# First mixer of a two-block transformer kernel: l2 lengths as per-partition factors, denominators from a column of ones, turned outputs issued inside other work

## What is computed

```python
qkv = silu(causal_conv(pa[..., :1536], conv_w))
qa = l2norm(q of 4 heads of 128) * 128 ** -0.5      # x * rsqrt(sum(x * x) + eps)
ka = l2norm(k of 4 heads of 128)
oa = gated_delta_rule(qa, ka, va, g, beta)          # needs (I + L)^-1, L from ka, beta, decays
oa = rmsnorm(oa, norm_a) * silu(z)
# second half: mLSTM
num = pmat @ v ; den = sum(pmat, -1)
ob = rmsnorm(num / max(abs(den), exp(-m)), norm_b) * o_gate
out = concat(oa, ob) @ w_out
```

## Time and profile before

| | |
|---|---|
| profiled execution | 1546.2 us |
| its span | 1544.9 us |
| median of three runs | 1546.9 us |
| mean granted clock of PE | 0.967 |
| PE busy | 95% of the span |
| DVE, ACT, POOL busy | 65%, 50%, 7% |

### The profile page before, as it was taken

One profiled execution on the slowest core, in us unless ns is written; L12 is line 12 of the kernel. 1 busy time (PEld: TensorE's weight loads), 2 busy tenths in 40 slices (PEclk: granted clock), 3 DMA queues, 4 the chain that ended last, 5 costly groups with the idle time before them and its releaser, 6 DMA issues.

```text
span 1544.9 us, 26112 instructions
## 1 busy us (share of the span) xinstructions
PE 1466.5 (95%) x10914; PEld 1388.4 (90%) x10914; DVE 1007.5 (65%) x1517; ACT 766.4 (50%) x1192; POOL 113.6 (7%) x104
## 2 busy tenths in 40 slices
PE   5999998999999898999999998999999998999999
PEld 5988987999997687999998787899999787899999
DVE  4746558664478756764476775677756676577763
ACT  4433345444356344444456767544346666544343
POOL 0002311110001001110000000011100000011100
PEclk8989998999999998999999998999999997999999
DMA  8531234655544324655555321556565412255563
GB/s 267 145 101 55 77 115 129 199 181 181 185 163 164 109 83 140 192 188 174 186 170 171 120 103 34 161 164 190 172 207 194 151 67 83 82 164 175 183 196 103
DMA packets 186389, 228.91 MB, mean 148 GB/s; under 512 B 5920, under 2 KB 161056, under 8 KB 186144
## 3 DMA queue, kind: packets, MB, share of 16 engines
q1 hardware_dynamic: 185264, 222.47, 44.9%
q0 software_dynamic: 1008, 4.77, 0.9%
HBM read 226.18 MB, written 1.05 MB: 147 GB/s over the span
## 4 chain that ended last, share of the span: by engine, by line
PE 70%; DVE 17%; ACT 8%; issue 3%; DMA 0%; POOL 0%; ACTq 0%; SPq 0%; DVEq 0%; POOLq 0%
PE bank L494 20%; PE bank L495 19%; PE bank L496 19%; DVE weights_low L788 6%; ACT weights_high L682 3%; PE bank L997 2%; PE bank L502 2%; ACT S L2050 2%; PE bank L1995 1%; DVE cv L2853 1%; PE bank L1974 1%; DVE S L2125 1%; DVE cv L2850 1%; DVE cv L1398 1%; DVE pad L2840 1%
## 5 line engine op out<-in xcount | busy, mean ns | idle before, releaser
L788 DVE TENSOR_TENSOR weights_low<-weights_raw,weights_high 128x1024 fp32r<-128x1024 f32 (+3 forms) x421 | 505.4, 1222 | 307.5 <-ACT weights_high L682 307.2
L682 ACT CAST weights_high<-weights_raw 128x1024 fp32r<-128x1024 f32 (+3 forms) x421 | 424.0, 1030 | 268.1 <-PE bank L496 267.8
L494 PE MATMUL bank<-hT_high,weights_high 128*128 128x256 f32 (+1 forms) x1672 | 482.9, 289 | 24.8 <-DVE hT_low L867 8.9
L495 PE MATMUL bank<-hT_low,weights_high 128*128 128x256 f32 (+1 forms) x1672 | 478.5, 286 | 0.0
L496 PE MATMUL bank<-hT_high,weights_low 128*128 128x256 f32 (+1 forms) x1672 | 478.2, 286 | 0.0
L494 PEld LDWEIGHTS bank<-hT_high,weights_high 128*128 128x128 f32 (+1 forms) x1672 | 325.0, 194 | 31.7 <-issue 16.8
L495 PEld LDWEIGHTS bank<-hT_low,weights_high 128*128 128x128 f32 (+1 forms) x1672 | 325.3, 195 | 0.6
L496 PEld LDWEIGHTS bank<-hT_high,weights_low 128*128 128x128 f32 (+1 forms) x1672 | 324.9, 194 | 0.6
L494 PE MATMUL bank<-aT_high,weights_high 128*128 128x256 f32 x864 | 241.2, 279 | 0.2
L495 PE MATMUL bank<-aT_low,weights_high 128*128 128x256 f32 x864 | 240.6, 279 | 0.0
L496 PE MATMUL bank<-aT_high,weights_low 128*128 128x256 f32 x864 | 240.3, 278 | 0.0
(11 more groups left out here) (414 smaller groups left out, 1818.5 us busy)
## 6 DMA issues: line engine op xcount, KB each, us to landing
weights_raw<-in_w_up SPq DMA_DIRECT2D x32, 1024.0 KB, 5.4
weights_raw<-in_w_down SPq DMA_DIRECT2D x32, 1024.0 KB, 4.9
weights_raw<-in_ffn_w_gate SPq DMA_DIRECT2D x22, 1024.0 KB, 5.3
weights_raw<-in_ffn_w_up SPq DMA_DIRECT2D x22, 1024.0 KB, 5.3
...
```

Of the source, the lines that this page charges most:

```text
L494: k.E.matmul(out, xh, wh, start=first, stop=False)
L495: k.E.matmul(out, xh, wl, start=False, stop=False)
L682: k.A.copy(w.halves(n)[0], w.raw_part(n)).then_inc(*k.s.weight_high(n))
L788: k.V.tensor_tensor(low, w.raw_part(n), high.bitcast(F32), ALU.subtract).then_inc(*k.s.weight_low(n))
```

## The change

- The order of the ten feature panels is changed: keys first (512, 768), then queries, and values last. The kinds (convolution or not) stay in the same places. `CONV_AB` keeps the convolution buffers and POOL's squares in that order.
- The length sums come in two groups of eight, for the keys behind f3 and for the queries behind f6. Each has its own root on ACT and its own reciprocal on DVE. `l2T`, its transposes and the row products are gone, and so are the products that scaled queries and keys. In their place the length of the key in the row of `ab` is multiplied into beta, the products key x key and key x query are multiplied by the other key's length by partition (`over_lengths`), and the query's length goes into the outputs of a.
- `abT` moves from behind f4 to behind f5, the scan and the turned maxima from behind f6 to behind f7.
- The values of b get a column of ones, so that the weighted values have the denominator in column 128. L1145 and its step go. There are now four such products in four banks, two heads in each.
- The turned outputs of b are issued ahead of the first u product, into buffers of their own (`m.bT`). Those of a are issued in the 28th step of the output panels, that is four steps before the second ends.

```diff
@@ -45,11 +45,14 @@
-FEATURES_AB = [("qkv_a", 0), ("qkv_a", 256), ("qkv_a", 512), ("qk_b", COL_QB), ("qkv_a", 768), ("qk_b", COL_QB + 256),
+FEATURES_AB = [("qkv_a", 512), ("qkv_a", 768), ("qkv_a", 0), ("qk_b", COL_QB), ("qkv_a", 256), ("qk_b", COL_QB + 256),
...
+CONV_AB = [4, 6, 0, 2, 8, 10]
@@ -392,13 +395,13 @@
-    m.qkv, m.qkb, m.both_gates, m.vb = cut("qkv", 12, SEQ), cut("qkb", 8, SEQ), cut("both_gates", 2 * NT * 512), cut("vb", NT, 512)
+    m.qkv, m.qkb, m.both_gates, m.vb = cut("qkv", 12, SEQ), cut("qkb", 8, SEQ), cut("both_gates", 2 * NT * 512), cut("vb", NT, 4, P + 1)
...
-    m.l2, m.l2T, m.em = cut("l2", NT, 8), cut("l2T", SEQ), cut("em", NT, 4)
+    m.l2, m.em = [cut("l2", NT, 4) for _ in range(2)], cut("em", NT, 4)
@@ -407,6 +410,7 @@
+    m.bT = pair("bT", 4, SEQ)
@@ -1019,34 +1023,32 @@
     yield
+    tensor_square_lengths(k, 4)
+    yield
...
     yield
+    tensor_square_lengths(k, 0)
...
     E.transpose(bank[:, 8:16], m.mxT[0:8, P:SEQ], k.ident[0:8, 0:8]).then_inc(*s.products("ab mcol"))
-    bank = k.banks.fill("ab l2")
-    for c in range(8):
+    yield
+
+
+def tensor_square_lengths(k, c0):
+
+    E, s, m = k.E, k.s, k.ab
+    bank = k.banks.fill(("ab l2", c0))
+    for c in range(c0, c0 + 4):
...
             a = (c % 2) * SEQ + t * P
-            mm = E.matmul(bank[:, t * 8 + c:t * 8 + c + 1], m.sq[:, c // 2, a:a + P], k.ones[:, 0:1], start=True, stop=True)
-    mm.then_inc(*s.products("ab l2"))
-    yield
-    E.wait_ge(*s.inverse.at("ab l2"))
-    tensor_transposes(k, "ab l2T", [m.l2[:, t, :] for t in range(NT)])
-    yield
-    select = k.const("select").rearrange("p (h n) -> p h n", h=12)
-    E.wait_ge(*k.banks.was_read("ab l2T"))
-    for c in range(0, 8, 2):
-        bank = k.banks.fill(("ab l2 row", c))
-        E.matmul(bank[:, 0:SEQ], select[0:8, c, :], m.l2T[0:8, :], start=True, stop=True)
-        E.matmul(bank[:, SEQ:512], select[0:8, c + 1, :], m.l2T[0:8, :], start=True, stop=True).then_inc(*s.products(("ab l2 row", c)))
-    yield
+            mm = E.matmul(bank[:, t * 4 + c - c0:t * 4 + c - c0 + 1], m.sq[:, c // 2, a:a + P], k.ones[:, 0:1], start=True, stop=True)
+    mm.then_inc(*s.products(("ab l2", c0)))
@@ -1106,12 +1108,13 @@
             tensor_by_heads(k, ("ab Q", lv, j), lambda hd: m.C[j][:, hd, :], lambda hd: m.M[j][:, hd, :])
-        if lv == 1:
-            tensor_denominators(k)
         if lv == 2:
+            for hd in range(4):
+                E.wait_ge(*k.banks.was_read(("ab P", hd)))
...
                 E.wait_ge(*k.banks.was_read(("ab", COL_VB, t)))
-            tensor_weighted(k, ("ab h b", 0), m.PT, m.vb, 0)
+            E.wait_ge(*s.padding.at("ab ones"))
+            tensor_weighted_b(k, 0)
@@ -1122,11 +1125,13 @@
-            tensor_weighted(k, ("ab h b", 1), m.PT, m.vb, 1)
+            tensor_weighted_b(k, 1)
...
+    E.wait_ge(*s.mixed.at("b"))
+    tensor_feature_major(k, "ab b", m.mixed_b, 4)
@@ -1134,21 +1139,21 @@
-def tensor_denominators(k):
-    E, m = k.E, k.ab
-    for hd in range(4):
-        E.wait_ge(*k.banks.was_read(("ab P", hd)))
-    bank = k.banks.fill("ab den")
-    for t in range(NT):
-        for hd in range(4):
+def tensor_weighted_b(k, t):
...
+    m, n = k.ab, P + 1
+    for pair in range(2):
+        bank = k.banks.fill(("ab h b", t, pair))
+        for i in range(2):
+            hd = 2 * pair + i
...
-                mm = E.matmul(bank[:, t * 4 + hd:t * 4 + hd + 1], m.PT[:, hd, (t + u) * P:(t + u + 1) * P], k.ones[:, 0:1], start=(u == 0), stop=(u == t))
-    mm.then_inc(*k.s.products("ab den"))
+                mm = k.E.matmul(bank[:, i * n:(i + 1) * n], m.PT[:, hd, (t + u) * P:(t + u + 1) * P], m.vb[:, u, hd, :], start=(u == 0), stop=(u == t))
+        mm.then_inc(*k.s.products(("ab h b", t, pair)))
...
-    E, m = k.E, k.ab
+    E, s, m = k.E, k.s, k.ab
@@ -1159,6 +1164,11 @@
+    yield
+    for _ in range(19):
+        yield
+    E.wait_ge(*s.mixed.at("a"))
+    tensor_feature_major(k, "ab a", m.mixed_a, 4)
@@ -1189,15 +1199,10 @@
             next(side, None)
-    E.wait_ge(*s.mixed.at("b"))
-    tensor_feature_major(k, "ab b", m.mixed_b, 4)
...
     for k0 in OUT_AB:
-        if k0 == 0:
-            E.wait_ge(*s.mixed.at("a"))
-            tensor_feature_major(k, "ab a", m.mixed_a, 4)
         ready = k.banks.was_read(("ab a" if k0 < 4 else "ab b", "T", k0 % 4))
-        tensor_deep_panel(k, "ab", held, m.top, k0, ("out_ab", k0, 0), ready, k0 == OUT_AB[0], k0 == OUT_AB[-1], behind)
+        tensor_deep_panel(k, "ab", held, m.top if k0 < 4 else m.bT, k0 % 4, ("out_ab", k0, 0), ready, k0 == OUT_AB[0], k0 == OUT_AB[-1], behind)
@@ -1248,21 +1253,31 @@
             A.copy(m.Q[j], per_head(k.banks["ab Q", lv, j][:, :], 4, P)).then_inc(*k.banks.read(("ab Q", lv, j)))
-        if lv == 1:
-            A.wait_ge(*s.products.at("ab den"))
-            A.activation(m.den, k.banks["ab den"][:, 0:8].rearrange("p (t n) -> p t n", t=NT), ACT.Abs).then_inc(*k.banks.read("ab den"))
+        if lv == 2:
+            scalar_denominators(k, 0)
...
             for t in range(NT):
-                A.wait_ge(*k.banks.was_read(("ab h b", t)))
+                for pair in range(2):
+                    A.wait_ge(*k.banks.was_read(("ab h b", t, pair)))
...
         yield
+        if lv == 2:
+            scalar_denominators(k, 1)
...
     A.copy(m.U[:, 0, :], k.banks["ab u 0"][:, :]).then_inc(*k.banks.read("ab u 0"))
-    yield
-    yield
+    scalar_feature_major(k, "ab b", 4, m.bT)
+    yield
+    yield
+
+
+def scalar_denominators(k, t):
+    for pair in range(2):
+        k.A.wait_ge(*k.s.products.at(("ab h b", t, pair)))
+        last = k.A.activation(k.ab.den[:, t, 2 * pair:2 * pair + 2], k.banks["ab h b", t, pair][:, P:2 * P + 2:P + 1], ACT.Abs)
+        last.then_inc(*k.s.logs(("ab den", t, pair)))
@@ -1277,45 +1292,42 @@
         n = k.w.first(("ab", 0, n0))
-        if i == 5:
+        if i in (4, 7):
+            c0 = {4: 4, 7: 0}[i]
+            A.wait_ge(*s.products.at(("ab l2", c0)))
+            A.activation(m.l2[c0 // 4], k.banks["ab l2", c0][:, 0:8].rearrange("p (t n) -> p t n", t=NT), ACT.Sqrt, bias=k.eps
+                         ).then_inc(*k.banks.read(("ab l2", c0)))
+        if i == 6:
...
             A.copy(m.abT[0:12, :], k.banks["ab abT"][0:12, 0:SEQ]).then_inc(*k.banks.read("ab abT"))
-        if i == 7:
-            A.wait_ge(*k.banks.was_read("ab l2"))
-            A.activation(m.l2, m.l2, ACT.Sqrt).then_inc(*s.root("ab l2"))
-        if i == 8:
-            A.wait_ge(*s.products.at("ab l2T"))
-            A.copy(m.l2T[0:8, :], k.banks["ab l2T"][0:8, 0:SEQ]).then_inc(*k.banks.read("ab l2T"))
...
             A.wait_ge(*s.conv.at((c, 1)))
-            A.activation(m.qkv[:, c:c + 2, :], m.cv[:, c // 2 % 2, :, :], ACT.Silu).then_inc(*s.silu(c))
+            A.activation(m.qkv[:, c:c + 2, :], m.cv[:, CONV_AB.index(c) % 2, :, :], ACT.Silu).then_inc(*s.silu(c))
...
     for n0, name, fn in SIDE_AB:
-        dst = {"zs": m.zs, "vb": m.vb, "og": m.og}[name]
+        dst = {"zs": m.zs, "vb": m.vb[:, :, :, 0:P], "og": m.og}[name]
...
                     A.wait_ge(*s.products.at(("ab", n0, t)))
-                    A.activation(dst[:, t, :], k.banks["ab", n0, t][:, :], fn, scale=m.inv[:, t:t + 1]).then_inc(*k.banks.read(("ab", n0, t)))
-    scalar_feature_major(k, "ab b", 4, [v[:, 4:8, :] for v in m.top])
+                    bank = k.banks["ab", n0, t][:, :]
+                    A.activation(dst[:, t], per_head(bank, 4, P) if name == "vb" else bank, fn, scale=m.inv[:, t:t + 1]).then_inc(*k.banks.read(("ab", n0, t)))
...
     A.copy(m.U[:, 1, :], k.banks["ab u 1"][:, :]).then_inc(*k.banks.read("ab u 1"))
-    A.wait_ge(*s.products.at(("ab h a", 0)))
-    A.copy(m.mixed_a[:, 0, :], k.banks["ab h a", 0][:, :])
-    A.activation(m.squares_a[:, 0, :], k.banks["ab h a", 0][:, :], ACT.Square).then_inc(*k.banks.read(("ab h a", 0)))
-    A.wait_ge(*k.banks.was_read(("ab h a", 1)))
-    A.activation(m.squares_a[:, 1, :], m.mixed_a[:, 1, :], ACT.Square).then_inc(*s.head_squares("a"))
+    for t in range(NT):
+        A.wait_ge(*k.banks.was_read(("ab h a", t)))
+        A.activation(m.squares_a[:, t, :], m.mixed_a[:, t, :], ACT.Square).then_inc(*s.head_squares("a" if t else "a begun"))
@@ -1358,8 +1370,11 @@
+    V.wait_ge(*k.banks.was_read(("ab l2", 4)))
+    V.reciprocal(m.l2[1], m.l2[1]).then_inc(*s.inverse("ab l2 k"))
+    V.wait_ge(*s.inverse.at("ab l2 k"))
...
-    V.tensor_copy(m.ab[:, :, 0:4], m.beta)
+    V.tensor_tensor(m.ab[:, :, 0:4], m.beta, m.l2[1], ALU.mult)
@@ -1422,12 +1438,18 @@
+    def over_lengths(to, key, hd):
...
+        bank, left = k.banks[key], m.AT[:, hd, :]
+        V.wait_ge(*s.products.at(key))
+        V.scalar_tensor_tensor(to[:, 0:SEQ], bank[:, 0:SEQ], m.l2[1][:, 0, hd:hd + 1], left[:, 0:SEQ], ALU.mult, ALU.mult)
+        V.scalar_tensor_tensor(to[:, SEQ:384], bank[:, SEQ:384], m.l2[1][:, 1, hd:hd + 1], left[:, SEQ:384], ALU.mult, ALU.mult
+                               ).then_inc(*k.banks.read(key))
...
```

(58 more changed lines are left out.)

20 lines of the change are left out of this document (7 added, 13 removed).

## The result

The changed kernel took 1524.7 us (median of four executions, 1521.0 to 1525.0) where the kernel before took 1546.9 beside it: a ratio of 0.985, with an interval from 0.983 to 0.987. The profiled execution took 1524.9, its span 1523.6, at a mean granted clock of 0.975. That is 21.3 us less span than before.

A forecast was written before the change was run, and what follows sets the result against it. PE, busy 95% of the span, was taken as the bound. Lengths 17.1, denominators 4.3 and turned outputs 2.1 us sum to 23.5 off 1546.2, giving 1522.7, stated as 1523; own range 1519 to 1526, wider range 1518 to 1532.

The forecast's parts named there:

- Lengths: Feature panels up to the side work's first select: length sums in two groups, row products and waits gone, 17.1 us saved.
- part 1's clock terms: Length rewrite in the features: 2.2 us at L1037, 2.8 under the next panel, 6.9 for row products and low clock.
- 2.8 lost to the clock: Feature panel following L1037: 8.5 us where 5.74 is usual; the 2.8 us goes if the clock holds.
- DVE and ACT's replay: Feature panels: DVE and ACT keep up with PE, all margins above 1 us; cost 0, bounds 0 and 3.
- The added table loads: ACT in the features: two more loads, 2.6 us of ACT; taken at no cost to PE.
- Denominators: Side work: a column of ones replaces L1145, 2.57 us, and the low clock behind it, 1.7; sum 4.3 us.
- Turned outputs: Around u products and output panels: moving both groups of transposes saves 2.1 us, 1.2 of it for b.
- Late stages keep their lengths: Stages behind the mixer: a change over 3 us would mean the sum over the mixer was not the whole story.
- the clock's fall behind the length groups: Features: one-column length sums still lower the clock, 1.7 to 5.2 us each fall; 1525 to 1533 us; chance 0.20.
- PE would starve for splits: Features: DVE and ACT become the bound, PE waits up to 3 us for weight splits; about 1526 us; chance 0.13.
- DMA didn't bind: Features: the rival had weights come too late for faster panels, gain not kept, about 1541 us; chance 0.05.
- The rival of a slower kernel: Features: clock falls at the first length group and a 36 us stretch doubles at 1.2 GHz; 1558 us; chance 0.02.

## Why the prediction was right

The forecast of 1523 held within 1.7 us (1524.7), or 2.2 against the profiled execution (1522.7 and 1524.9). It was carried by the sum: the three parts were put at 23.5 us and made 24.1 against the first trace of the kernel before, 22.3 against its repeat. By the medians of its three comparisons the change is worth 22.2, 22.9 and 21.8 us. That the number came out within 1.7 us is in part luck, since the late stages alone moved by 4.3. The sum's steps went so:

- **Lengths, 17.1 expected, 17.5 measured.** The first length group filled the wait at the split: f5 starts at 58.55 with about 0.2 us lost at its split instead of 1.43 (59.15 on the old scale, where the panels started 0.6 later; the sum had 59.2). The low clocks under f7 and the row products are gone. The gap of 0.3 expected at the scan didn't come: the scan ended at 77.71 and PE was there at 77.97. The groups took 1.71 us each up to the next panel, the 1.7 of the sum; the 1.84 of their rows counts the last record to its end, and it overlaps with the next.
- **The size of part 1's clock terms was less certain than I wrote.** I read windows of 12 and 8 us from one execution; the low stretches in them are 10.2 and 6.8 us. The repeat had 1.8 us less to give: against it part 1 gained 15.7 where 17.1 was summed. My own range had room for it, as shifts of later stages, but the term "2.8 lost to the clock" should have carried that doubt itself.
- **DVE and ACT's replay** held within 0.5 us at the points I read, all on the old scale: f6's split done at 63.6 (64.0 said), f4's convolution at 63.5 (64.0), f6's at 74.0 (74.4). The timelines of ACT and DVE show the two points behind it:

```profile
58.12 1.28 ACT L1298 ACT_TABLE_LOAD   x1
59.41 0.27 ACT L1298 ACTIVATE l<-bank,consts 128x8 f32<-128x8 f32 x1
```

```profile
73.42 0.68 DVE L1401 TENSOR_TENSOR pad<-bank,factor 128x512 f32<-128x512 f32 x1
...
77.04 0.67 DVE L1575 TENSOR_TENSOR_SCAN mxT<-abT 12x256 f32<-12x256 f32 x1
```

- **The added table loads, cost 0.** The root starts 0.01 us behind the end of its load (59.41 behind 58.12 + 1.28), and 0.02 in the earlier trace rows and in the run with two more loads (71.16 behind 69.86 + 1.28). The drain that the Trainium skill gives in "ScalarE: Activation LUTs", section "What ACT_TABLE_LOAD costs", stands in none of these traces.
- **Denominators, 4.3 expected, 4.1 measured** against the kernel before, 4.3 with the old ones put back. No wait came from the four banks.
- **Turned outputs, 2.1 expected, 2.5 measured.** Group b gave 1.3 for 1.2: the gap ahead of the output panels was 0.51 where the sum had 0.25, and the 0.4 expected at the second u product didn't come. Group a has no gap and gave 1.2 for 1.0.
- **"Late stages keep their lengths"** was named as the test, and they missed it by 4.3 us. As far as the repeats and variants tell, the sum over the mixer was still what the change did, and the 4.3 belongs to the execution. It is also why the forecast came out low: the two traces compared above differ by 25.6 us up to the feed-forward block, of which 1.4 (0.6 ahead of f1, 0.8 behind the output panels) are not the change's either, since the repeat of the kernel before has the changed kernel's lengths there; 4.3 went the other way.

Of the rivals, the clock's fall behind the length groups didn't happen in the changed kernel's three traces. Part of the ground on which I gave it 0.20 was weak, though: of the three traces with the idle 2.61 us, two have a fall there, and of the five with L1145 one has none behind it. That PE would starve for splits found 0.2 us at f5 and no other gap at a split. DMA didn't bind: PE lost no time over the features with 150 GB/s moved. The rival of a slower kernel took the time at 1.2 GHz as double; in these traces panel records start 0.213 us apart at the low clock and 0.12 at the full one, 1.8 times.
